# Decoder trunk on one core: the last mixer unit's products by row tile, and two blocks of the mixer in another order

## The reference, cut to what matters

```python
for l in range(DEPTH):                                  # DEPTH = 2
    h = rmsnorm(x, norm1_g[l])
    x = x + token_mixers(h, ...)                        # four mixers, sigmoid gates, merged @ w_out
    h = rmsnorm(x, norm2_g[l])
    x = x + hierarchical_moe(h, ...)                    # 4 groups x 8 experts, top-1 group, top-2 inside
return rmsnorm(x, norm_f_g)

# token_mixers
proj = h @ w_in                                         # 7076 columns, 4096 of them gate logits
y_b = chunked_sgu(ub, vb, ...)                          # u * (tril(W_s) LayerNorm(v) + b)
y_c = stick_breaking_attention(qc, kc, vc)
merged = sum over n of gates[:, :, n] * (branches[n] @ w_branch[n])
return merged @ w_out                                   # 1024 x 1024

# hierarchical_moe: softmax over h @ w_router_group + b, logits h @ w_router_expert + b,
# then for every expert silu(h @ w_g) * (h @ w_u) @ w_d, weighted
```

## Time and profile before

| | us |
|---|---|
| median of three runs | 894.63 (892.83 to 897.02) |
| the profiled execution, whole | 894.49 |
| its span, first to last instruction | 892.8 |
| PE busy | 827.9 (93%) |
| DVE busy | 529.8 (59%) |
| ACT busy | 387.1 (43%) |
| POOL busy | 117.1 (13%) |

### The profile page before, as it was taken

One profiled execution on the slowest core, in us unless ns is written; L12 is line 12 of the kernel. 1 busy time (PEld: TensorE's weight loads), 2 busy tenths in 40 slices (PEclk: granted clock), 3 DMA queues, 4 the chain that ended last, 5 costly groups with the idle time before them and its releaser, 6 DMA issues.

```text
span 892.8 us, 20363 instructions
## 1 busy us (share of the span) xinstructions
PE 827.9 (93%) x8763; PEld 665.2 (75%) x8763; DVE 529.8 (59%) x1067; ACT 387.1 (43%) x669; POOL 117.1 (13%) x169
## 2 busy tenths in 40 slices
PE   7999899999999998877899998999999999987884
PEld 7998788887886775664589977888789876664652
DVE  5768688667555555423376777985656455544433
ACT  5546777545422222111275667674544222221113
POOL 2840101212000000000056001022200000000000
PEclk9999999999999999988999999999999999999988
DMA  9966445489979999999997463455996999999994
GB/s 308 389 214 174 158 142 178 153 360 359 366 274 418 420 419 419 420 421 420 401 368 282 155 217 101 153 181 217 406 329 270 406 420 420 419 419 419 420 420 178
DMA packets 63838, 281.49 MB, mean 315 GB/s; under 512 B 5088, under 2 KB 7216, under 8 KB 39168
## 3 DMA queue, kind: packets, MB, share of 16 engines
q1 hardware_dynamic: 62464, 278.45, 80.0%
q0 software_dynamic: 800, 1.40, 1.1%
q10 hardware_dynamic: 480, 0.28, 0.1%
HBM read 279.06 MB, written 1.05 MB: 314 GB/s over the span
## 4 chain that ended last, share of the span: by engine, by line
PE 67%; DMA 18%; issue 5%; SPq 3%; POOL 3%; DVE 2%; ACT 2%; DVEq 0%; ACTq 0%; POOLq 0%
PE ps L486 13%; PE ps L488 12%; PE ps L487 12%; PE ps L818 9%; DMA ring<-in_w_exp_up 6%; DMA new_pair<-in_w_exp_up 6%; PE ps L805 5%; PE ps L832 4%; DMA ring<-in_w_exp_down 3%; PE ps L913 3%; DMA late<-in_w_exp_down 3%; SPq L382 2%; POOL wide L1545 1%; PE ps L824 1%; PE ps L453 1%
## 5 line engine op out<-in xcount | busy, mean ns | idle before, releaser
L1658 DVE TENSOR_TENSOR split_lo<-ring,split_hi 128x1024 fp32r<-128x1024 f32 (+1 forms) x142 | 196.1, 1418 | 41.2 <-ACT split_hi L1131 40.0
L486 PE MATMUL ps<-split_hi,hT_hi 128*128 128x512 f32 (+2 forms) x416 | 162.0, 389 | 0.9 <-DVE hT_lo L1668 0.9
L1131 ACT ACTIVATE split_hi<-ring 128x1024 fp32r<-128x1024 f32 (+1 forms) x144 | 145.6, 1048 | 34.4 <-PE ps L488 33.2
L487 PE MATMUL ps<-split_lo,hT_hi 128*128 128x512 f32 (+2 forms) x416 | 158.4, 381 | 0.0
L488 PE MATMUL ps<-split_hi,hT_lo 128*128 128x512 f32 (+2 forms) x384 | 145.8, 380 | 0.0
L2070 DVE TENSOR_TENSOR wsT<-mb,ps 32x64 f32<-32x64 f32 x256 | 54.9, 215 | 142.3 <-ACT mb L1341 139.7
L1341 ACT ACTIVATE mb<-ps 128x64 f32<-128x64 f32 x64 | 14.3, 223 | 245.1 <-PE ps L818 245.1
L486 PEld LDWEIGHTS ps<-split_hi,hT_hi 128*128 128x128 f32 x416 | 78.9, 190 | 18.9 <-issue 3.7
L487 PEld LDWEIGHTS ps<-split_lo,hT_hi 128*128 128x128 f32 x416 | 78.9, 190 | 13.1
L488 PEld LDWEIGHTS ps<-split_hi,hT_lo 128*128 128x128 f32 x384 | 72.7, 189 | 13.3
L1562 POOL TENSOR_TENSOR idx<-idx,wt 128x128 f32<-128x128 f32 x32 | 12.1, 399 | 391.0 <-PE ps L838 307.4
(11 more groups left out here) (278 smaller groups left out, 1319.6 us busy)
## 6 DMA issues: line engine op xcount, KB each, us to landing
ring<-in_w_in SPq DMA_DIRECT2D x52, 1024.0 KB, 10.2
ring<-in_w_exp_gate SPq DMA_DIRECT2D x45, 1024.0 KB, 24.5
ring<-in_w_exp_up SPq DMA_DIRECT2D x45, 1024.0 KB, 26.0
late<-in_w_exp_down SPq DMA_DIRECT2D x39, 1024.0 KB, 26.5
ring<-in_w_exp_down SPq DMA_DIRECT2D x16, 1024.0 KB, 26.6
new_pair<-in_w_exp_gate SPq DMA_DIRECT2D x10, 1024.0 KB, 18.1
new_pair<-in_w_exp_up SPq DMA_DIRECT2D x10, 1024.0 KB, 20.2
late<-in_w_exp_gate SPq DMA_DIRECT2D x9, 1024.0 KB, 24.4
```

The source lines that it names most:

```text
L486: mm(dst, st[0], mv[0], start=start, stop=False, skip_group_check=True)
L487: mm(dst, st[0], mv[1], start=False, stop=False, skip_group_check=True)
L1131: A(half_view(split_hi[:, v % SPLITS, :], v), raw_half(v, l), ACT.Copy).then_inc(hi_done, 1)
L1658: V.tensor_tensor(half_view(split_lo[:, v % SPLITS, :], v), raw_half(v, l), half_view(split_hi[:, v % SPLITS, :], v).bitcast(F32), ALU.sub ...
```

## The change

`mid_mm` and `x_mid` are raised once more per layer. On PE, unit 15 stands ahead of the wait for `vn_done`; `in_half(62)` stands ahead of `m_transposes(0)`; unit 35 and the router part are written out by row tile. On ACT one wait ahead of the table load is gone. DVE's additions are split and interleaved.

```diff
-    ... mid_mm=1, wide_mm=4, x_mid=2,
+    ... mid_mm=2, wide_mm=4, x_mid=3,
...
                     pv(vc, 0, 7)
+                    in_unit(15, 9)
                     pe.wait_ge(*L(vn_done, 1))
                     for g in range(NG):
                         ins = mm(ps[:, 6, P * g:P * g + P], wsT[:, g, :], vn[:, :, HD * g:HD * g + HD],
                                  start=(g == 0), stop=True, skip_group_check=True)
                     ins.then_inc(sgu_mm, 1)
-                    in_unit(15, 9)
                     in_half(32, 9)
...
+                    in_half(62, 21)
                     m_transposes(0)
-                    in_unit(31, 21)
+                    in_half(63, 21)
                     pe.wait_ge(*L(xT_lo, 7))
...
-                    wide_unit(35, 22, m_tile(3), False, True)
-                    pe.wait_ge(router_loaded, 16 * 2 * (l + 1))
-                    keep_warm(4, 7)
-                    for t in range(TT):
-                        pe.wait_ge(*L(x_mid, t + 1))
-                        ...                                     # eight transposes of tile t
-                    for t in range(TT):
-                        ...                                     # eight router matmuls of tile t
+                    for k in range(2):
+                        pe.wait_ge(*L(lo_done, 2 * NU - 1 + k))
+                        for hf in range(2):
+                            ins = last_product(k, hf, 0)
+                    ins.then_inc(mid_mm, 1)
+                    for k in range(2):
+                        ins = last_product(k, 0, 1)
+                    ins.then_inc(mid_mm, 1)
+                    last_product(0, 1, 1).then_inc(half_used, 1)
+                    pe.wait_ge(*L(x_mid, 1))
+                    mid_transposes(0, 0)
+                    mid_transposes(0, 1)
+                    last_product(1, 1, 1).then_inc(half_used, 1)
+                    pe.wait_ge(router_loaded, 16 * 2 * (l + 1))
+                    router_logits(0, 0)
+                    pe.wait_ge(*L(x_mid, 2))
+                    mid_transposes(1, 0)
+                    router_logits(0, 1)
+                    pe.wait_ge(*L(x_mid, 3))
+                    mid_transposes(1, 1)
+                    router_logits(1, 0)
+                    router_logits(1, 1)
                     keep_warm(11, 7)
...
-                    act.wait_ge(*L(half_used, 2 * NU - 1))
                     preload_sqrt()
                     for t in range(TT):
-                        act.wait_ge(*L(x_mid, t + 1))
+                        act.wait_ge(*L(x_mid, 2 * t + 1))
                         square_of_x(t)
...
+                    dve.wait_ge(*L(mid_mm, 1))
+                    mid_add(0, 0)
+                    mid_add(0, 1).then_inc(x_mid, 1)
+                    dve.wait_ge(*L(mid_mm, 2))
+                    mid_add(1, 0).then_inc(x_mid, 1)
+                    dve.wait_ge(gain_out, 1)
+                    mid_scaled(0)
+                    mid_scaled(1)
+                    dve.wait_ge(*L(half_used, 2 * NU))
+                    mid_add(1, 1).then_inc(x_mid, 1)
+                    mid_scaled(2)
```

More of the change, by code:

```diff
@@ L103 @@
     conv_y=1, ln_var=1, ln_root=1, vn_dve=1, vn_done=1, sgu_mm=1, yb_done=1, yT_mm=3, yT_hi_out=4, yT_lo_out=4,
-    la_mm=2, la_max=2, la_exp=2, gate_prod=8, gate_sum=6, mid_mm=1, wide_mm=4, x_mid=2,
+    la_mm=2, la_max=2, la_exp=2, gate_prod=8, gate_sum=6, mid_mm=2, wide_mm=4, x_mid=3,
     route_mm=2, gmax=1, gexp=1, emax=1, eexp=1, member_ok=1,
@@ L554, in wide_unit @@
                             pe.wait_ge(*L(lo_done, v + 1))
[L555 to L559, removed]
+                            for n, (hf, t) in enumerate((hf, t) for hf in range(2) for t in range(TT)):
                                 if first_ and v % 2 == 0 and t == 0:
@@ L563, in wide_unit @@
                                             first_ and v % 2 == 0, last_ and v % 2 == 1)
-                                if final_half and n == 1:
-                                    ins.then_inc(mid_mm, 1)
-                                elif first_ and last_ and v % 2 == 1 and n == 1:
+                                if first_ and last_ and v % 2 == 1 and n == 1:
                                     ins.then_inc(wide_mm, 1)
@@ L767, in _ @@
                     wide_unit(34, 22, m_tile(2), False, False)
-                    wide_unit(35, 22, m_tile(3), False, True)
-                    pe.wait_ge(router_loaded, 16 * 2 * (l + 1))
-                    keep_warm(4, 7)
-                    for t in range(TT):
-                        pe.wait_ge(*L(x_mid, t + 1))
-                        for c in range(C):
-                            ins = nc.tensor.transpose(ps[:, 4 + 2 * t + c // 4, P * (c % 4):P * (c % 4) + P],
-                                                      x[:, t, P * c:P * c + P], ident[:])
-                            if c % 4 == 3:
-                                ins.then_inc(xT_mm, 1)
@@ L780, in _, with last_product, mid_transposes @@
-                    for t in range(TT):
-                        for c in range(C):
-                            if c % 4 == 0:
-                                pe.wait_ge(*(L(xT_lo, 10), L(xT_lo, 11), L(xT_lo, 12), L(xT_hi, 10))[2 * t + c // 4])
+                    def last_product(k, hf, t):
+                        return three(ps[:, 2 * hf + t, :], m_tile(3)(k, t), w_tile(2 * NU - 2 + k, 0, 512 * hf, 512),
+                                     False, k == 1)
+                    def mid_transposes(t, q):
+                        for c in range(4 * q, 4 * q + 4):
+                            ins = nc.tensor.transpose(ps[:, 4 + 2 * t + q, P * (c % 4):P * (c % 4) + P],
+                                                      x[:, t, P * c:P * c + P], ident[:])
+                        ins.then_inc(xT_mm, 1)
@@ L784, in _, with router_logits @@
+                    def router_logits(t, q):
+                        pe.wait_ge(*(L(xT_lo, 10), L(xT_lo, 11), L(xT_lo, 12), L(xT_hi, 10))[2 * t + q])
+                        for c in range(4 * q, 4 * q + 4):
                             ins = mm(ps[:, t, 0:NG + NE], hT[:, c, P * t:P * t + P], wr[:, c, :],
                                      start=(c == 0), stop=(c == C - 1), skip_group_check=True)
-                        ins.then_inc(route_mm, 1)
+                        if q == 1:
+                            ins.then_inc(route_mm, 1)
@@ L1954, in _, with mid_add, mid_scaled @@
                     lo(35)
[L1955 to L1960, removed]
                     V.memset(rt[:, 96:112], -TAKEN)
-                    dve.wait_ge(gain_out, 1)
-                    for k in range(3):
+                    def mid_add(t, hf):
+                        xs = x[:, t, 512 * hf:512 * hf + 512]
+                        return V.tensor_tensor(xs, xs, bank(2 * hf + t), ALU.add)
+                    def mid_scaled(k):
                         t, c0 = k // 2, 4 * (k % 2)
```

## The result

The changed kernel took 889.49 us (median of 5, 889.04 to 890.83) against 895.38 for the kernel before beside it: a ratio of 0.9935, 95% interval 0.9915 to 0.9955. Run once more on another occasion, beside the experiments, it took 890.71 against 894.56, ratio 0.9962 (0.9949 to 0.9976). So the gain is 5.9 us by the first pair of medians and 3.9 by the second, and the two intervals together reach from 2 to 7.6; 5.7 had been forecast. The profiled execution took 890.83 (span 889.1), 3.7 less than the one of before.

The account below looks back on a forecast made before the run. Bound: PE's chain up to the eighth expert's load, then DMA. Unit 15 4.8, merged -0.2, unit 35 and router 0.8, layer 1's clock 0.3 sum to 5.7 off 894.63: 888.9 us, range 887.0 to 891.7.

Parts of the forecast that it names:

- Unit 15: Gating: unit 15 ahead of the vn_done wait gains PE 2.75, held to DVE's 2.4 a layer, 4.8 us in all.
- a new wait: Gating, before the zexp transposes (L596): PE waits 1.5 us anew, for ACT's Exp.
- rival (a): Before L596: the clock falls in the new 1.5 us wait, costing 1.6 a layer; chance 0.13.
- the wait that was forecast there: Unit 21: PE waits for a DVE split near 147.6, its gain falling to DVE's 2.4.
- Rival (b): Before unit 21: PE meets DVE sooner and keeps only 1.3 a layer, 891.1 us; chance 0.13.
- the 1.6: Gating, behind the POOL stall: the low clock (0.50) cost PE 1.6 us.
- `merged`: Its transposes past half 62: unit 32's splits come later, PE waits; cost 0.1 a layer, 0.2 us in all.
- (d): At merged: the stall on gate_sum goes as well, up to 0.6 a layer more, 887.7 us; chance 0.09.
- Unit 35 and the router: Layer's tail by row tile: logits start at 242.8 against 243.18, gaining 0.4 a layer, 0.8 us in all.
- The clock term of 0.3 in layer 1: Behind layer 1's router: about 0.6 of low-clock time reached the ranks; half counted as saved, 0.3 us.
- whatever shortens the chain up to the eighth expert's load shortens the kernel by as much: Experts' stage: it ends a fixed number of bytes after that load, so gains ahead count fully in each layer.
- the rest costs nothing: ACT's removed wait and SP's loads 0.9 later are covered by idle time; uncovered, the loads would cost 0.9 a layer.

Follow-up runs that it names:

- Gate between: Kernel with the gate_sum wait behind half 62, plus DVE's step 2 gating product between the two instructions of sparse_logits(1): 889.49 us, ratio 0.9938.
- filler: Kernel before with ten keep_warm matmuls in the stall ahead of the wait for vn_done, real work in the old order: 892.25 us, ratio 0.9963.
- tail alone: Kernel before with only unit 35 and the router written by row tile: 894.22 us, ratio 0.9990.

## Why the prediction was right

**Unit 15.** The mechanism held: 2.76 at the transposes against 2.75, a new wait of 1.40 against 1.5, clock 1.00 behind it (rival (a) didn't occur), DVE's idle time at `yT_lo` gone. PE kept 2.56 at unit 21 against 2.4, so 5.1 for 4.8. Where the missing 0.2 went was put wrong. It goes at the new wait itself, where the 12 transposes up to half 33 take 1.41 (114.70 to 116.11) for 1.23 (116.49 to the first matmul of half 33 in the kernel before, below); from there to half 43 PE took 32.33 after and 32.31 before. Unit 21's split is ready 0.05 ahead of PE in both, but PE loses only 0.08 there, so the wait that was forecast there did not show; DVE itself is 2.55 earlier at that point, which would have held PE to about the same. Gate between does not settle it, since it made PE wait one half earlier. Why the transposes are slower behind the new wait stays open. Rival (b), PE meeting DVE sooner, didn't occur either. PE, kernel before:

```profile
117.72 0.47 PE L486 MATMUL ps<-split_hi,hT_hi 128*128 128x512 f32 x1
```

**What the clock was worth.** The sum took the 1.6 as certain in both layers of before. The price is right (filler, tail alone), but in six such stalls without filler the clock fell in five, once for longer (15.55). The unprofiled executions behind the median before may be of either kind, which, by an estimate from the 1.6, leaves this term uncertain by about 1 us.

**`merged`.** Cost 0.18 a layer for 0.1. The stall on half 62's first matmul stayed, as the order showed, so (d) didn't occur; moving that wait by one line takes it away and is worth 0.87 a layer by the trace.

**Unit 35 and the router.** 0.3 to 0.4 a layer for 0.4, the last quarter released by ACT with a wait of 0.42 for 0.5. The clock term of 0.3 in layer 1 came out as 0.47 in the profile, but in the repeat the clock fell there (3.96): it is a matter of executions (the ranks stretch took 3.68 or more in 4 of 20 cases with the new tail, in 5 of 8 with the old), not a fixed gain.

**What follows the load.** The step that failed is that whatever shortens the chain up to the eighth expert's load shortens the kernel by as much, and with it "the rest costs nothing". Up to layer 1's eighth load the two profiles differ by 5.78, as summed; behind it 1.1 was lost in both profiles of the changed kernel, and 0.3 to 0.7 in four of its relatives with the new tail. In layer 0 the stretch from the load to layer 1's L598 took 284.99 to 285.05 in four of the ten profiles with the new tail, the repeat among them, and 284.26 to 284.59 in all others. So the time behind the load is fixed to about 1 us only. In the two profiles of the changed kernel that is more than the 0.7 that the new order of the tail had won; the tail alone gained 0.6 by its median, which its interval does not tell from nothing.

**Luck.** The forecast of 888.9 lies 0.6 below the first median and 1.8 below the second. That the first came so near is in part luck: the kernel before was 0.75 slower beside it than in the runs that the forecast started from, unit 15 brought 0.3 more than summed, and the loss behind the load was not in the sum at all.

## What to carry to other kernels

Put ready work ahead of a wait and see first what the clock does behind it: here filler alone gave over half of the gain at that wait, by the trace, without moving any real work. When a chain of one engine bounds a stage, look for its idle gaps upstream and move independent work into them; and set a wait directly ahead of what needs it, not one block earlier. Gains that add up at a marker in the middle should be followed to the end, since time can be lost again behind it: here 1.1 us of 5.8.

## What the runs showed of the hardware

A stall of PE of 2.56 to 2.57 us was followed by a clock of 0.50 in five of six cases and of 1.00 in the sixth (layer 1 of tail alone, 2.57). A DVE `tensor_scalar` of four elements a partition took 1.13 us for 0.17 beside a POOL addition, while a reduction of 1024 elements beside it took its usual 1.21; POOL's addition took 2.40 beside the reduction and 3.33 beside splits (gate between). A stop of PE that the profile gives as 0.61 idle cost 0.87: matmuls stand 0.23 apart but are drawn 0.39 long, so 1.00 lay between two starts, and the first ones behind it were 0.1 slower. PE can stand 0.5 to 0.8 us with no releaser in the experts' stage while DMA is full; with eight matmul records more ahead of it the stalls in layer 1 were gone from the profile (0.12 left), but the median stayed.
